# Blocks of the feed-forward operands laid 2,080 bytes apart in SBUF

## What is computed

```
def swiglu(u, w_in, w_out):
    gate, up = jnp.split(u @ w_in, 2, axis=-1)
    return (jax.nn.silu(gate) * up) @ w_out
...
        h = h + 0.5 * ml[:, 2][:, None] * swiglu(
            modulate(rmsnorm(h, norm_g[li, 0]), ml[:, 0], ml[:, 1]), ffn_w_in[li, 0], ffn_w_out[li, 0])
        hc = hc + 0.5 * mc[:, 2][:, None] * swiglu(
            modulate(rmsnorm(hc, norm_g[li, 0]), mc[:, 0], mc[:, 1]), ffn_w_in[li, 0], ffn_w_out[li, 0])
...
        h = h + 0.5 * ml[:, 8][:, None] * swiglu(
            modulate(rmsnorm(h, norm_g[li, 2]), ml[:, 6], ml[:, 7]), ffn_w_in[li, 1], ffn_w_out[li, 1])
    return rmsnorm(h, final_g)
```

## Time and profile before

| | |
|---|---|
| median of 2 executions | 2872.07 us |
| profiled execution | 2869.9 us, span 2868.0 us |
| TensorE busy | 2812.3 us, 98% of the span |
| weight loads busy (beside the matmuls) | 2376.3 us, 83% |
| VectorE busy | 1612.3 us, 56% |
| ScalarE busy | 987.0 us, 34% |
| GpSimd busy | 219.0 us, 8% |
| mean granted TensorE clock | 0.991 |

### The profile page before, as it was taken

One profiled execution on the slowest core, in us unless ns is written; L12 is line 12 of the kernel. 1 busy time (PEld: TensorE's weight loads), 2 busy tenths in 40 slices (PEclk: granted clock), 3 DMA queues, 4 the chain that ended last, 5 costly groups with the idle time before them and its releaser, 6 DMA issues. The chain is left out here.

```text
span 2868.0 us, 42535 instructions
## 1 busy us (share of the span) xinstructions
PE 2812.3 (98%) x15728; PEld 2376.3 (83%) x15728; DVE 1612.3 (56%) x2068; ACT 987.0 (34%) x1443; POOL 219.0 (8%) x373
## 2 busy tenths in 40 slices
PE   6999999999999999999999999998999999999998
PEld 3788888888888888888888888878988888888887
DVE  4567767667676752223226666655675555555444
ACT  3222222222222222111214555544354444444443
POOL 0000000000000000000101103555120000000001
PEclk8999999999999999999999999999999999999999
DMA  9866676677888856655663666685556666666664
GB/s 377 302 209 218 195 224 218 199 220 245 315 307 300 313 191 198 191 187 171 192 195 97 170 188 185 202 259 173 161 177 191 190 190 190 190 190 191 190 189 142
DMA packets 410336, 604.63 MB, mean 211 GB/s; under 512 B 52960, under 2 KB 303840, under 8 KB 401520
## 3 DMA queue, kind: packets, MB, share of 16 engines
q1 hardware_dynamic: 361824, 419.52, 47.3%
q10 hardware_dynamic: 48400, 183.63, 19.1%
HBM read 560.02 MB, written 43.02 MB: 210 GB/s over the span
## 5 line engine op out<-in xcount | busy, mean ns | idle before, releaser
L1989 DVE TENSOR_TENSOR wl<-raw,wh 128x1024 fp32r<-128x1024 f32 x638 | 785.0, 1232 | 928.2 <-ACT wh L1511 927.0
L1511 ACT CAST wh<-raw 128x1024 fp32r<-128x1024 f32 x638 | 667.5, 1047 | 1465.6 <-PE ps L785 1043.0
L784 PE MATMUL ps<-xl,wh 128*128 128x512 f32 (+1 forms) x2560 | 968.6, 378 | 0.0
L783 PE MATMUL ps<-xh,wh 128*128 128x512 f32 (+1 forms) x1904 | 722.9, 380 | 0.8 <-DVE wl L1989 0.7
L785 PE MATMUL ps<-xh,wl 128*128 128x512 f32 (+1 forms) x1904 | 717.0, 377 | 0.0
L784 PEld LDWEIGHTS ps<-xl,wh 128*128 128x128 f32 x2560 | 482.3, 188 | 89.8
L783 PEld LDWEIGHTS ps<-xh,wh 128*128 128x128 f32 x1904 | 359.1, 189 | 75.6 <-issue 8.9
L785 PEld LDWEIGHTS ps<-xh,wl 128*128 128x128 f32 x1904 | 358.6, 188 | 66.3
L791 PE MATMUL ps<-x,wh 128*128 128x512 f32 x1408 | 379.7, 394 | 1.7 <-DVE x L2059 1.7
L2171 DVE SCALAR_TENSOR_TENSOR acc<-abuf,cT,acc 128x1024 f32<-128x1024 f32 x300 | 371.4, 1280 | 16.0 <-DMA abuf<-in_w_ada 15.7
L791 PEld LDWEIGHTS ps<-x,wh 128*128 128x128 f32 x1408 | 241.6, 189 | 34.3 <-issue 2.0
(11 more groups left out here) (298 smaller groups left out, 2451.2 us busy)
## 6 DMA issues: line engine op xcount, KB each, us to landing
raw<-in_ffn_w_in SPq DMA_DIRECT2D x704, 256.0 KB, 3.3
raw<-in_ffn_w_out SPq DMA_DIRECT2D x176, 512.0 KB, 3.7
abuf<-in_w_ada ACTq DMA_DIRECT2D x64, 1024.0 KB, 6.8
abuf<-in_w_ada ACTq DMA_DIRECT2D x96, 512.0 KB, 4.0
xl<-d_h ACTq DMA_DIRECT2D x80, 512.0 KB, 3.3
ada_t<-in_ada SPq DMA_DIRECT2D x64, 512.0 KB, 9.5
raw<-in_w_in SPq DMA_DIRECT2D x128, 256.0 KB, 3.5
raw<-in_w_out SPq DMA_DIRECT2D x32, 512.0 KB, 4.7
```

The costliest lines, as they stand in the source:

```text
L783: mm(out, ah, bh, start=first, stop=False, skip_group_check=reopened)
L784: mm(out, ah, bl, start=False, stop=False, skip_group_check=reopened)
L1511: nc.scalar.copy(wh[:, t % HL, :], raw[:, t % RAW, :]).then_inc(hi_done, 1)
L1989: tt(tl, raw[:, t % RAW, :], th.bitcast(F32), ALU.subtract).then_inc(lo_done, 1)
```

## The change

A constant `PITCH = NTOK + 8` (520 columns, 2,080 bytes) becomes the length of a block in `xh`, `xl`, `x2`, `ha`, `hb` and `hc`; the instructions use the first 512 columns of each. The starts of all buffers modulo 512 are as before (a new spacer `apart5` sees to that behind `yl`), and so is the step of the stationary slices. Block `k` of a buffer now lies 32 times `k` further than block 0 modulo 512: distances 0, 32, 64 up to 480 for `xh` and `xl`, and 64 plus 32 times `k` for the blocks of FFN2. `hth`, `htl`, `yh`, `yl` and the weights keep their layout. To make room, `yt` and `osq` (of the mixing stage) lie in another place, under `x2`. Numbers, operand sizes and types, engines and waits of all instructions are unchanged. The destination of the fetch of hidden blocks is now two pieces of 2,048 bytes per partition and no longer one of 4,096.

```diff
+PITCH = NTOK + 8
...
-            xh = sb("xh", [P, KT, NTOK], F32R, stack=both)
-            xl = sb("xl", [P, KT, NTOK], F32R, stack=both)
+            xh, xl = (sb(n, [P, KT, PITCH], F32R, stack=both)[:, :, 0:NTOK] for n in ("xh", "xl"))
...
-            ha = sb("ha", [P, HID_A, 2, SEQ], F32R, stack=hid_a)
+            ha = sb("ha", [P, HID_A, PITCH], F32R, stack=hid_a)
         yh = sb("yh", [P, KT, SEQ], F32R)
         yl = sb("yl", [P, KT, SEQ], F32R)
+        sb("apart5", [P, KT * (PITCH - NTOK)])
         with ExitStack() as pooling:
...
+            yt = sb("yt", [P, SEQ], stack=pooling)
+            osq = sb("osq", [P, 2, P], stack=pooling)
...
-        x2 = sb("x2", [P, KT, 2, SEQ], F32R)
-        x2h, x2l = x2[:, :, 0, :], x2[:, :, 1, :]
+        x2 = sb("x2", [P, KT, PITCH], F32R)
+        x2h, x2l = x2[:, :, 0:SEQ], x2[:, :, SEQ:2 * SEQ]
...
-                hb = sb("hb", [P, HID_B, 2, SEQ], F32R, stack=hid_b)
+                hb = sb("hb", [P, HID_B, PITCH], F32R, stack=hid_b)
...
-                hc = sb("hc", [P, K_FF - HID_A - HID_B, 2, SEQ], F32R, stack=hid_c)
+                hc = sb("hc", [P, K_FF - HID_A - HID_B, PITCH], F32R, stack=hid_c)
...
-                yt = sb("yt", [P, SEQ], stack=two)
-                osq = sb("osq", [P, 2, P], stack=two)
...
-                    return mm(ps[:, bank + q, SEQ:2 * SEQ], wl[:, t % HL, w], b[:, 0, :], start=False, stop=False)
+                    return mm(ps[:, bank + q, SEQ:2 * SEQ], wl[:, t % HL, w], b[:, 0:SEQ], start=False, stop=False)
...
-                    i = block_products(4 * p, range(4), t, kk, x2[:, kk], kk == 0, kk == KT - 1)
+                    i = block_products(4 * p, range(4), t, kk, x2[:, kk, 0:2 * SEQ], kk == 0, kk == KT - 1)
...
-                return block_products(4 * (n % 2), qs, T_DOWN2 + n * DOWN2_TILES + kk // TILE_K, kk, hid2(kk, 1)[:, 0],
+                return block_products(4 * (n % 2), qs, T_DOWN2 + n * DOWN2_TILES + kk // TILE_K, kk, hid2(kk, 1)[:, 0, 0:2 * SEQ],
...
-                nc.scalar.copy(hid2(2 * p, 2)[:, :, 0, :], hf[:, :, 0:SEQ]).then_inc(F[1]["hh_done"], 1)
+                nc.scalar.copy(hid2(2 * p, 2)[:, :, 0:SEQ], hf[:, :, 0:SEQ]).then_inc(F[1]["hh_done"], 1)
...
-                tt(h2[:, :, 1, :], hf[:, :, 0:SEQ], h2[:, :, 0, :].bitcast(F32), ALU.subtract
+                tt(h2[:, :, SEQ:2 * SEQ], hf[:, :, 0:SEQ], h2[:, :, 0:SEQ].bitcast(F32), ALU.subtract
```

## The result

The changed kernel took 2910.82 us (median of 2 executions, 2907.73 to 2913.91) against 2872.07 us. The ratio is 1.014, 95% interval 1.0123 to 1.0156. The sign of the forecast was right and its size was not: +39 us where I had +15, just outside the stated range (2840 to 2908).

The account below looks back on a forecast made before the run. TensorE's matmul steps were taken to bound the kernel: +13.5 (first stage) + 4.6 (second stage) - 1.7 (heads) = +16.4 us on the profiled 2869.9 us, 2886.3 us, so 2887 us for a median; range 2840 to 2908 us.

Parts of the forecast that it names:

- What bounds the kernel: Both feed-forward stages: time is the number of matmuls times TensorE's step; the other engines wait for it.
- The signs named for the forecast: First stage 1080 to 1530 us: some 1965 matmuls, not 1987; FFN2's 400 us: 1150 pairs; xh block 0: 226.7 ns.
- the first term: First feed-forward stage: 5880 matmuls leave distance 0 and take 229 ns, 2.3 ns more each, +13.5 us.
- its two rows: Trace steps of 512 columns: six decay-tile matmuls at 230 ns each, and FFN2 at distance 64 at 229 ns.
- My own upper bound for one step: First stage: some 236 ns if every step were as dear as the worst that recur.
- The second term: Second feed-forward stage: 2112 pairs at all multiples of 32, 347.7 ns a pair, +4.6 us; bounds -11 and +21 us.
- The third: Heads: 768 pairs leave distance 0 with its 350 ns for a middle of 347.7 ns, -1.7 us.
- That the distance doesn't matter: Rival: steady states form from the order and sizes of the matmuls; 2870 to 2877 us, chance 0.20.
- That the odd multiples of 32 are good: Rival, faster side: the fixed part falls at these distances, 2851 us, or vanishes, 2811 us; chance 0.28.
- That they are dear: Rival: odd multiples of 32 collide, costing 236 ns a step and 356 ns a pair; 2915 us, chance 0.13.
- second way: First stage, way up: each change of block breaks the steady state once, 352 blocks costing 7.4 us.
- Hidden costs: Fetch into xl in shorter pieces: lands in 3.3 us, has 16 us; ScalarE's and VectorE's writes stand in long waits.

## Why the prediction was half right

**What bounds the kernel** was read rightly: TensorE's step, with no wait in either stage. The count of matmuls that leave distance 0 (5880) stands too; with it and the measured steps the span's difference comes out to 1.3 us. The signs named for the forecast came, more strongly: 1948 matmuls in the stretch of 450 us for some 1965, 1142 pairs in the 400 us for 1150, and block 0 at 226.7 ns after its first step.

**The step that failed** is the size of the first term: "That both are above 226.7 and near one another is why I take 229". It was 232.1 on the way up and 232.15 in the ring, so the term was 33.3 us and not 13.5. Three things were wrong with its two rows. The decay tiles load 32 columns of weights, not 128; the run with loads of 64 shows that a shorter load changes both the cost and which distances are dear, so these rows stood for another operation. The six matmuls shown are of two blocks, at distances 0 and 384, and not at the four from 0 to 384; modulo 256 these are 0 and 128. At distance 128, full loads take 233.3 ns where I had read 230 across the decay tile. And FFN2's 229 ns at 64 is one distance, in a stream of another order; in the first stage 64 has 229.9 and is after 0 the best of the eight. That the two rows agreed said nothing of the other distances. My own upper bound for one step, 236 ns, held for the mean of every block of the changed kernel (234.2 at most); the range should have reached to a mean near it over all 5880 and not over half.

**The second term**, the second stage: forecast +4.6, measured +9.4 us by its steps and +7.6 by the run with that part alone. The middle between 345.4 and 350 was taken as if these were the ends; seven of the sixteen distances lie above 351. **The third**, the heads: forecast -1.7, measured near nought, 0.1 us in the 220 us compared above.

**The rivals.** That the distance doesn't matter is refuted by the constant 128 and by the moved weights. The rule that stood behind this rival goes with it: a load that is read through a port of its own and takes nothing from the running matmul (the Trainium skill, "TensorE: Matmul & The Clock Gate", "Step-by-step: what each phase is for") leaves no room for a kernel that is 1.0124 times as long when only `xh` and `xl` lie 128 bytes further on. That the odd multiples of 32 are good is refuted (232.5 to 234.2 ns). That they are dear is true and its time, 2915 us, was the nearest; but as a mechanism it was wrong too, since 128 and 192 are as dear. The "second way", 7.4 us from rhythms that break at each block, turned out small: a block at distance 0 is entered with one step of 233 ns, 6 ns instead of 21.

**Hidden costs** were hidden as forecast: the fetch lands in 3.6 us, and no wait for it shows in the trace of either kernel.

The statement on distances was modulo 512. The traces show a period of 256 in the first stage, and none in the second (348.8 ns a pair at 64, 342.8 at 320).

## What to carry to other kernels

Where matmuls follow each other without a gap, the distance of the moving operand from the stationary one is part of the tuning, worth 3 to 4% of a step here (226.7 to 233.6 or 236.5 ns): find a good one and keep it for all blocks, as a varying one gets the mean of good and bad. A pitch that sweeps the distance is a poor layout but a cheap instrument, since one profile then gives the step at 16 distances. Carry a distance over only to matmuls with the same columns, the same length of load and the same order, and measure it there: a uniform 28 was as good as 0 on the way up, and not in the ring.

## What the hardware showed that I had not expected

- In a stream of like matmuls, the step of 512 columns against a full load has a lowest mean of 226.7 ns, met at distances 0, 28, 60, 240 and 256, and rises to 236.5 ns at 4. Four bytes decide.
- In that stream the pattern repeats after 256 bytes to 0.1 ns, and holds from one kernel and chip to another: the way up takes 232.4 ns at 128 on one chip and at 384 on another.
- The floor is the same with half the load, but the distance at which it is met moved from 0 to 160. Together with the earlier trace rows, where 256 and 512 columns have the same 13.3 ns over their columns at distance 0, this says that the fixed part is due neither to the load's length nor to the moving operand's. What it is stays open. It is not the least for every matmul: where the two kinds alternate at 28, those of 512 columns take 227.8 ns and those of 256 take 115.4, which is 14.5 and 8.8 ns over their columns.
- A uniform distance and the same distance among others agree within 1 ns on the way up of the first stage (232.4 and 233.3 at 128), but not where 512 and 256 columns alternate (346.7 and 351.1 ns a pair at 192 modulo 256).
